# Attention values with V stationary: two heads in the column halves of the array, outputs turned back

## What is computed

```python
def fox_attention(q, k, v, log_f):          # 8 heads
    logits = einsum('bqhd,bshd->bhqs', qb, k) * scale
    logits = where(causal, logits + bias, -inf)
    p = softmax(logits, axis=-1)
    return einsum('bhqs,bshd->bqhd', p, v)

def dsa_attention(q, k, v, iq, ik, iw, k_top):   # 8 heads, keys chosen by top_k
    ...
    p = softmax(logits, axis=-1)
    return einsum('bhqk,bqkhd->bqhd', p, v_sel)

def hybrid_mixer(h, ...):
    proj = h @ w_in
    ...
    y = concatenate([rms_norm(o_d, dsa_norm_g), rms_norm(o_f, fox_norm_g)], axis=-1)
    return y @ w_out

x = x + g1 * hybrid_mixer(modulate(rms_norm(x), sh1, sc1), ...)
x = x + g2 * swiglu(modulate(rms_norm(x), sh2, sc2), w_gate, w_up, w_down)
return rms_norm(x, final_norm_g)
```

## Time and profile before

| | before |
|---|---|
| median of 3 runs | 1415.51 us (1409.33 to 1415.94) |
| span of the profiled execution | 1410.2 us |
| TensorE busy | 1348.2 us, 96% |
| VectorE, ScalarE, GpSimd busy | 73%, 49%, 57% |
| attention, first logits to last value product | 367.6 to 650.6 us |
| mean granted TensorE clock | 0.991 of full |

### The profile page before, as it was taken

The page is one execution under the profiler, slowest core; times in us unless marked ns, Lnnn a source line. Parts: engine busy times, 40 slices in busy tenths (PEclk is TensorE's granted clock), DMA queues, the critical chain, the costliest instruction groups (busy, mean ns, idle before and its releaser), DMA issues.

```text
span 1410.2 us, 20288 instructions
## 1 busy us (share of the span) xinstructions
PE 1348.2 (96%) x7043; PEld 1152.2 (82%) x7043; DVE 1027.3 (73%) x1599; ACT 692.2 (49%) x1372; POOL 803.2 (57%) x536
## 2 busy tenths in 40 slices
PE   1999999999999999999999899999999999999996
PEld 1988788888899999888888688888888888788885
DVE  4463779999685788996558777655566665579998
ACT  6523345563467667765335443444333333454545
POOL 0251312323336433580006798889998984798985
PEclk9999999999899999999999999999999999999998
DMA  9131222352333867432311233333223333998874
GB/s 384 43 97 60 90 68 75 105 167 91 115 81 103 261 196 208 123 117 90 120 46 45 60 112 113 112 112 112 97 98 112 113 108 132 369 381 293 279 240 161
DMA packets 126286, 200.59 MB, mean 142 GB/s; under 512 B 10637, under 2 KB 60997, under 8 KB 125162
## 3 DMA queue, kind: packets, MB, share of 16 engines
q1 hardware_dynamic: 126186, 199.30, 42.7%
HBM read 156.99 MB, written 42.27 MB: 141 GB/s over the span
## 4 chain that ended last, share of the span: by engine, by line
PE 82%; DVE 7%; issue 3%; DMA 2%; POOL 2%; ACT 2%; SPq 1%; ACTq 0%; DVEq 0%; POOLq 0%
PE PS L2047 21%; PE PS L2048 21%; PE PS L2049 21%; PE PS L2243 7%; PE PS L2207 4%; PE PS L2226 2%; DMA ada<-in_ada_w_dram 1%; PE PS L2228 1%; POOL WSf L937 1%; PE PS L2231 1%; DVE AS L1913 1%; DVE LP L1701 1%; POOL WS L949 1%; DVE junk L1731 1%; ACT F L1208 1%
## 5 line engine op out<-in xcount | busy, mean ns | idle before, releaser
L949 POOL TENSOR_TENSOR WS<-WSf,WS 128x512 fp32r<-128x512 f32 x109 | 161.6, 1490 | 9.1 <-ACT WS L1227 9.1
L1227 ACT CAST WS<-WSf 128x512 fp32r<-128x512 f32 x110 | 68.5, 623 | 196.2 <-POOL WSf L937 195.5
L937 POOL TENSOR_TENSOR WSf<-rawg 128x512 f32<-128x512 f32 x55 | 78.1, 1420 | 139.3 <-PE PS L2049 134.8
L2243 PE MATMUL PS<-Vn,PT 128*128 128x64 f32 x1152 | 144.2, 271 | 0.1
L2243 PEld LDWEIGHTS PS<-Vn,PT 128*128 128x128 f32 x1152 | 140.6, 194 | 0.9 <-ACT PT L1153 0.3
L2047 PE MATMUL PS<-yh,WS 128*128 128x512 f32 (+2 forms) x360 | 139.2, 387 | 1.5 <-DVE yl L1827 1.5
L2049 PE MATMUL PS<-yh,WS 128*128 128x512 f32 (+2 forms) x360 | 138.7, 385 | 0.0
L2048 PE MATMUL PS<-yl,WS 128*128 128x512 f32 (+2 forms) x360 | 138.7, 385 | 0.0
L2047 PE MATMUL PS<-BS,AS 128*128 128x512 f32 x308 | 120.4, 391 | 3.2 <-DVE BS L1918 2.1
L2049 PE MATMUL PS<-BS,AS 128*128 128x512 f32 x308 | 119.9, 389 | 0.0
L2048 PE MATMUL PS<-BS,AS 128*128 128x512 f32 x308 | 119.8, 389 | 0.0
(11 more groups left out here) (321 smaller groups left out, 3732.0 us busy)
## 6 DMA issues: line engine op xcount, KB each, us to landing
rawb<-in_w_down_dram SPq DMA_DIRECT2D x132, 256.0 KB, 4.8
rawa<-gu_scratch SPq DMA_DIRECT2D x77, 256.0 KB, 4.7
gu_scratch<-GS SPq DMA_DIRECT2D x55, 256.0 KB, 4.7
raw<-in_w_in_dram SPq DMA_DIRECT2D x24, 512.0 KB, 3.9
rawg<-in_w_gate_dram SPq DMA_DIRECT2D x22, 512.0 KB, 4.3
rawu<-in_w_up_dram SPq DMA_DIRECT2D x22, 512.0 KB, 4.5
ada<-in_ada_w_dram SPq DMA_DIRECT2D x8, 1024.0 KB, 14.8
qk_scratch<-stage SPq DMA_DIRECT2D x32, 256.0 KB, 2.2
```

The lines of the kernel that those rows point to most:

```text
L937: pool.tensor_tensor(WSf[m % N_SLOT][:], left(i, mat, a), left(i, mat, b), ALU.add if sign > 0 else ALU.subtract).then_inc(ws_sum, 1)
L949: pool.tensor_tensor(lo, WSf[m % N_SLOT][:] if b else left(i, mat, a), hi.bitcast(F32), ALU.subtract).then_inc(ws_ready, 1)
L2243: last = pe.matmul(PS[:, 6 + hd % 2, t * DH:(t + 1) * DH], PT[:, u % 2, j * P:(j + 1) * P], Vn[(hd // 4) % 2][:, j, cols], start=j == 0, s ...
```

## The change

The value products swap their operands. V is stationary (128 keys by 64 columns), and the transposed probabilities move. Two heads, a **pair** `p` with heads `2p` and `2p + 1`, write to PSUM partitions 0 to 63 and 64 to 127 of the same columns. The query tiles go in couples `g` (tiles `2g` and `2g + 1`), so that one matmul moves 256 columns; the odd tile stands first, and the last key block moves it alone (128 columns). The output has V's columns on partitions; ScalarE copies it to `O` (`evac_output`), TensorE transposes it back (group `"O"` in `turn`), and VectorE normalises out of PSUM to `O` again. With `r = s - 16 p` for the step counted from the pair's first unit, the four blocks of value products stand at r = 12, 14, 16 and 18, the copies at 15 and 19, the turns back at 16 and 20, the normalisations at 17 and 21 (r = 16 and more is in the next pair's first head).

```diff
+V_PARTS = 2
+PAIR = 2 * TT
+VALUE_AT = {PAIR * p + at: (p, g) for p in range(N_PAIR) for g, at in enumerate((12, 14, 16, 18))}
+EVAC_AT = {PAIR * p + at: (p, half) for p in range(N_PAIR) for half, at in enumerate((15, 19))}
+BACK_AT = {PAIR * p + at: (p, half) for p in range(N_PAIR) for half, at in enumerate((16, 20))}
+NORM_AT = {PAIR * p + at: (p, half) for p in range(N_PAIR) for half, at in enumerate((17, 21))}
+LAST_STEP = PAIR * (N_PAIR - 1) + 21
...
+            def values(p, g):
+                t = 2 * g + 1
+                pe.wait_ge(tp_ev, ev_count["T", PAIR * p + TT + t, len(halves(P * (t + 1))) - 1])
...
+                for j in range(t + 1):
+                    n = 2 * P if j < t else P
+                    for a in range(2):
+                        rows = slice(a * DH, (a + 1) * DH)
+                        last = pe.matmul(PS[rows, 6 + g // 2, (g % 2) * 2 * P:(g % 2) * 2 * P + n], Vn[p % 2][:, j, rows],
+                                         pt_read(2 * p + a, g, j), start=j == 0, stop=j == t)
...
+                held = ("O", N_PAIR - 1, 0) if g == LAST_BACK else plan[n - 2] if n >= 2 else None
+                if g == LAST_BACK:
+                    pe.wait_ge(ot_ok, 2 * N_PAIR - 1)
+                elif held and held[0] == "O":
+                    pe.wait_ge(on_done, back_count[held])
+                elif held:
+                    pe.wait_ge(tp_ev, ev_count[held])
...
+                if g[0] == "O":
+                    p, half = g[1], g[2]
+                    pe.wait_ge(ot_ok, 2 * p + half + 1)
+                    for i in range(4):
+                        last = pe.transpose(dst[:, i * P:(i + 1) * P], O[:, 4 * half + (i ^ 1), pair_cols(p)], ident[:])
...
+            def evac_output(p, half):
+                act.wait_ge(pv_pe, N_GROUP * p + 2 * half + 2)
+                act.copy(O[:, 4 * half:4 * half + 4, pair_cols(p)], PS[:, 6 + half, :].rearrange("p (t c) -> p t c", c=P)
+                         ).then_inc(ot_ok, 1)
...
+            def normalise(p, half):
+                dve.wait_ge(tp_pe, group_no[g] + 1)
...
-                for i, dst in enumerate((Qd[b], Kd[b])):
+                if hd >= 1:
+                    sp.wait_ge(k_lo, hd)
+                    sp.wait_ge(q_lo, hd)
+                for i, dst in enumerate((Qd, Kd)):
```

More of the change, by code:

```diff
@@ L221, in transposes_plan @@
     order = []
-    for s in range(UNITS + 2):
-        hd, t = divmod(s, TT)
+    for s in range(LAST_STEP):
         if s in ANGLE_UNITS:
@@ L246, in build, with turn_bank @@
     group_no = {g: n for n, g in enumerate(plan)}
+    ev_count = {g: sum(e[0] != "O" for e in plan[:n + 1]) for n, g in enumerate(plan)}
+    back_count = {g: sum(e[0] == "O" for e in plan[:n + 1]) for n, g in enumerate(plan)}
+    n_ev = sum(e[0] != "O" for e in plan)
+    def turn_bank(g):
+        return 6 if g == LAST_BACK else 4 + group_no[g] % 2
     with ExitStack() as ctx:
@@ L375, in build, with pt_home, pt_write, pt_read @@
         PS = ctx.enter_context(nc.psum_tensor("PS", [P, 8, BANK], F32))
+        def pt_home(hd, g, j):
+            if hd % 2:
+                return pt_b[g % 2], 0
+            first, rest = pt_a_rest.get(g, (TT, None))
+            return (rest, first) if j >= first else (pt_a[g], 0)
+        def pt_write(hd, t, j0, j1):
+            home, first = pt_home(hd, t // 2, j0)
+            at0 = (j0 - first) * 2 * P + (1 - t % 2) * P
+            if j1 - j0 == 1:
+                return home[:, at0:at0 + P]
+            return home[:, at0:at0 + (2 * (j1 - j0) - 1) * P].rearrange("p (j c) -> p j c", c=P)[:, ::2, :]
+        def pt_read(hd, g, j):
+            home, first = pt_home(hd, g, j)
+            at0 = (j - first) * 2 * P
+            return home[:, at0:at0 + (2 * P if j <= 2 * g else P)]
         def mod_weights(n):
@@ L590, in _, with load_values @@
                 load_piece(n)
[L591 to L597, removed]
+            def load_values(p):
+                cols = slice((p % 4) * 2 * DH, (p % 4 + 1) * 2 * DH)
+                if p >= 2:
+                    sp.wait_ge(pv_pe, N_GROUP * (p - 1))
+                for part in range(V_PARTS):
+                    tiles = slice(part * TT // V_PARTS, (part + 1) * TT // V_PARTS)
+                    src = v_dram[p // 4].rearrange("(t p) n -> p t n", p=P)[:, tiles, cols]
+                    sp.dma_start(Vn[p % 2][:, tiles, :], src).then_inc(qkv_in[p % 2], 16)
             def load_qk(hd):
                 b, first, row = hd % 2, 0 if hd < NH else 2, hd % NH * DH
[L601 to L604 removed]
+                if hd >= 1:
+                    sp.wait_ge(k_lo, hd)
+                    sp.wait_ge(q_lo, hd)
+                for i, dst in enumerate((Qd, Kd)):
                     for half in range(2):
@@ L645, in _ @@
                         load_piece(PIECES * (ch + 1) + t)
+                    if ch == 6 and t == 4:
+                        load_qk(1)
                 if ch == 4:
@@ L672, in _ @@
             sp.wait_ge(marks_free, 1)
-            for part in range(V_PARTS):
-                load_values(1, part)
+            load_values(0)
+            load_values(1)
             n_mod = 0
@@ L2248, in _ @@
             pe.wait_ge(sign_cnt, len(SIGN_TILES) * BISECT)
-            for s in range(UNITS + 3):
-                hd, t = divmod(s, TT)
+            for s in range(LAST_STEP):
                 if s < UNITS:
@@ L2259, in _ @@
                         turn(("T", s - 2, b))
-                if s >= 3:
-                    values(s - 3)
-            pe.wait_ge(tp_ev, len(plan))
+                if s in BACK_AT:
+                    turn(("O", *BACK_AT[s]))
+                if s in VALUE_AT:
+                    values(*VALUE_AT[s])
+            pe.wait_ge(tp_ev, n_ev)
+            pe.wait_ge(on_done, 2 * N_PAIR - 1)
             def out_part(q, ks, first, last):
```

216 lines of the change are left out of this document (126 added, 90 removed).

## The result

The change makes the kernel **slower**: 1442.05 us median of 4 runs (1437.64 to 1445.39) against 1414.49 (1409.33 to 1415.94), a ratio of 1.0209 [1.0176, 1.0241]. The forecast was 1436, from 1398 to 1490. The profiled execution has a span of 1441.1 us, 30.9 more than before.

The account below looks back on a forecast made before the run. The prediction took TensorE, busy 96% of the span, as the bound before the change. To the 1410.2 us span it added 10.6 for attention's terms and 15 for clock falls: 1436 us, range 1398 to 1490.

Parts of the forecast that it names:

- TensorE's cost of the value products: With the two heads fully overlapped, value products take 8.3 us a pair, against 15.6 before the change.
- Rival 1: The two heads' value products do not overlap: 8.3 us a pair more, 66 in all, 1487 to 1500; chance 0.22.
- Stalls (a), (b), (c): TensorE waits in P: turn back for ScalarE's copy 1.4 us, transposes for normalisation 1.1, last block for a copy 0.3.
- Going to column halves and back: TensorE's switching into and out of column halves around value products, 64 times: +3 us, from 0 to 6.
- P: Steps r = 12 to 18 of a pair, with all value products: TensorE's 16.6 us plus 2.8 of stalls, 19.4.
- Part Q: Steps r = 19 to 27 of a pair, without value products: 14.6 us with modulation, 13.4 without; TensorE idles 4 to 5.
- TensorE's sum: TensorE's work for a pair of heads falls from 32.8 to 26.4 us; outside 26 to 27 the forecast is wrong.
- "Moves that I cost at nothing": Single-buffered `Qd` and `Kd`, smaller V loads, moved memset, bias load and modulation groups, late `w_out` splits: 0 us.
- The clock: TensorE's idling in Q brings five clock falls, 5 us each, two in five of that hidden: +15 us, 0 to 45.
- The two ends: Attention's first twelve steps get 3 us shorter, its end after the last transposes 3 us longer.
- heads 6 to 11: Three pairs with modulation products, each 34.0 us against 32.8 before: +3.6 us in all.
- Rival 2: ScalarE and VectorE run ahead during blocks, stalls vanish, clock stays: pairs 30.0 or 31.2 us, kernel about 1397; chance 0.17.

Follow-up runs that it names:

- Experiment 2: Changed kernel with turns back at r = 17 and 20, normalisations at r = 18 and 20: 1419.74 us.
- 5: Changed kernel with the later turns back and normalisations of Experiment 2, and two modulation loads a head ahead of queries and keys: 1409.23 us.
- Experiment 9: On 5, the output copies and turns back left out, the first normalisation at r = 16, results wrong: 1406.83 us.
- experiment 3: Changed kernel with, in each block, all value products of the first head before those of the second: 1483.62 us.
- experiment 7: Changed kernel with the two long value blocks cut in two, turns back at r = 17 and 21, and most modulation products moved to P: 1425.93 us.

## Why the prediction was right, and where it was off

The likeliest case came: slower, 1442 against 1436. Some terms were right, others only in their sum, and how near the number came is in part luck.

- **TensorE's cost of the value products: right.** 0.21 us a couple of 256 columns, 0.11 for 128, some 7.7 us a pair for 8.3. Rival 1 is refuted. Its price of 66 us was not measured: one head after the other costs 41, with a part still side by side.
- **Stalls (a), (b), (c): right** in place and size: 1.4, 1.1 and 0.3 forecast, 1.39, 1.04 and 0.21 measured. Experiment 2 shows that they and the next one cost the time.
- **Going to column halves and back: too small.** At r = 16 the last of four transposes starts at 510.16. The first products follow after 0.20 rather than 0.11, the second couple after 0.26 rather than 0.21, and behind the last couple the logits start after 0.21 rather than 0.11. That is 0.25 a block, 32 blocks, some 8 us, against +3 in the sum and 6 as its end. It lies in P, where TensorE is the bound: P took 20.9, 21.0 and, in heads 11 and 12, 22.5 in the three pairs without a fall, for 19.4 forecast. The Trainium skill (TensorEngine Tiling (Array Packing), key properties) names a drain at a change of mode, without a price; the trace agrees with it, at about 0.12 a change, though it doesn't show that a drain is what takes the time.
- **Part Q: too long, and bound by the wrong engine.** I had 14.6 with four modulation products, set by VectorE's sum, and 13.4 without, set by ScalarE's. It takes 13.4 with four products and with two, though it now holds a wait of 1.1 for the second normalisation, which I had not seen; its second half goes at ScalarE's pace. Where a modulation load was late, Q took 16.1 and 14.5. A P and a Q without a fall or a late load add up to 34.3 or 34.4, for 34.0: two errors that cancel.
- **TensorE's sum: inside its test by one reading, outside by the other.** The prediction calls itself wrong if the sum is not 26 to 27 us a pair. TensorE's busy time is 28.6 (10.55 + 18.01), outside. Busy time also counts the modelled end of the last instruction before each wait; by the spacing of starts I estimate 26.4 - 0.6 for the products + 1.0 for the four blocks' changes = 26.8. The other test held: P and Q from steps 44, 60 and 76 on take 37.8, 37.0 and 39.3 us, none under 32.8. TensorE's busy share in attention fell to 81% (247.7 of 304.8 us from 372 us on), as forecast.
- **"Moves that I cost at nothing": wrong for the single `Qd` and `Kd`.** I looked at when Q and K land, and not at what stands behind `load_qk` in SP's list. The modulation loads do, and they came late: 6 us in the changed kernel, 10 once the stalls were gone, of which some 7 are clock.
- **The clock: falls right in number, their price too high.** Five were forecast and five came, 3.4 to 6.8 us long. The clock lost by them is 10.2 us, and the first fall costs 3.4 less than before, so attention loses 6.8 more and not 15. Another 5.1 is lost behind attention, where I had none.
- **The two ends: each off, -2.5 together where I had 0.** The first twelve steps give 8.8 us (for 3), 3.4 of it the shorter first fall of the clock; I had counted 92 instructions of value products there, and the trace has 74. The end takes 6.3 (for 3); the parts that I listed for it come to 5.4 - 3.5 = 1.9.
- **Heads 2 to 5 and 12 to 15.** Steps 12 to 44 took 7.1 us more, where I had 0 for heads 2 to 5; two falls are 3.4 of it. Steps 92 to 124 took 5.2 more, for +4.

For heads 6 to 11 the forecast was +3.6. Steps 44 to 92 took 114.1 us for 98.3, +15.8. The three parts Q took 44.0 us, for 43.8 forecast (14.6 each): two of them were lengthened by late loads, one was short. The three parts P took 70.1, for 58.2: there are the 11.9 that were missed, 5.0 of them clock lost by two falls (at 474 and 535.5), some 3 the column halves. I haven't split the remainder.

The sum of the forecast for attention, 25.6, meets the measured 25.6 by luck. Without the clock the forecast was +10.6 and the measured time is +18.8; the clock was to cost 15 and costs 6.8.

**Rival 2** decided, as the prediction had it, on the stalls. They did not vanish by themselves, since no engine ran ahead. When moved away (5), the best pairs come to 32.6 and 32.7, and the kernel to 1409. That is still 12 us above the 1397 of that rival: P is 18.6 to 20.7 and not 16.6, in part by the cost of the halves and by waits of up to 0.9 for ScalarE's copies.

**Where the expected gain went.** TensorE's sum for a pair fell, by its busy time, from 32.8 to 28.7 (10.83 + 17.85 in 5). VectorE's is 28.5 there (12.53 + 15.99). Before, TensorE alone was the bound. Now it is the bound in P only. In Q it waits for the others, and what sets the pace there is ScalarE for the second half; VectorE, with 1.8 us less to do, left Q as long as it was. What bounds the first half of Q was not tried. Experiment 9 takes a copy of 0.6 us out of ScalarE's first half of Q, and Q gets 0 to 0.2 us shorter; no run made ScalarE's work in the second half shorter, so its part there rests on the traces alone.

## What to carry to other kernels

Packing two heads into the array's column halves does halve the time of their products, here to 0.21 us a couple. Where the other engines are only some 15 to 30% below the first, what counts afterwards is where the saved time lies: products that stood in every step kept TensorE busy while it waited for the others, and gathered in blocks they don't. The engine with the largest busy share in a stretch need not be the one that sets its pace: look for two stretches in which its work differs, and compare their lengths. Before an operation is put between a producer and a consumer that share a bank in turn (here the turn back), ask for the step at which its input is surely there; moving it and its normalisations by a step was worth 25 us, nearly the whole difference of 28 between the kernels. When a load gets a later wait, read the issue list below it: everything behind it becomes later too.

## What the runs showed of the hardware that I had not expected

- TensorE began instructions of the other column half three to four ahead of their order in the program, without being told to (experiment 3: 528.70 for `PTb`, with `PTa2r` still starting until 529.24; so in each of its blocks).
- Entering and leaving the column halves takes about 0.25 us for a block of products.
- A modulation product on VectorE took 5.82 us beside a TENSOR_TENSOR of GpSimd and 1.28 by itself (experiment 7); a mere change of step can bring the two together.
- Idle TensorE time can be paid twice: each of the five falls of the granted clock came at a single wait of 1.2 to 2.0 us (such as those at 473.73 and 535.66) and slowed the block behind it. But such a wait does not always bring a fall: of the eight equal waits of 1.39 us before a turn back, two did (at 398 and 474 us).
